# ScalarE loads one table set for both logarithm and exponential at the head of stages with norms

## The chip, the cores and the metric

The kernel runs on one core of a Trainium2 chip. A core has five engines with their own instruction streams: TensorE (PE in the profile), VectorE (DVE), ScalarE (ACT), GpSimd (POOL) and SyncE (SP), which here only issues transfers. The metric is the device time of one execution in microseconds; it is compared by the median of several runs.

## The reference, cut to what matters

One inference step runs two decoder layers on 512 prompt tokens and 64 sample tokens (8 requests of 8), 576 tokens in all, with a model width of 1024. Layer 0 mixes Mamba-2 heads with sparse attention heads, layer 1 mixes gated DeltaNet heads with dilated attention heads, and each layer ends in an MLP with a hidden width of 4096. What bears on the change is how often a root mean square stands in it:

```python
def rmsnorm(x, w):
    xf = x.astype(jnp.float32)
    y = xf * lax.rsqrt(jnp.mean(xf * xf, axis=-1, keepdims=True) + RMS_EPS)
    return (y * w.astype(jnp.float32)).astype(x.dtype)

def l2norm(x):
    xf = x.astype(jnp.float32)
    return xf * lax.rsqrt(jnp.sum(xf * xf, axis=-1, keepdims=True) + 1e-6)

# per layer
h = rmsnorm(x, norm_mix_pre);  x = x + rmsnorm(mixer(h), norm_mix_post)
h = rmsnorm(x, norm_mlp_pre);  x = x + rmsnorm(mlp(h), norm_mlp_post)
# mlp(h) = square(relu(h @ w1)) @ w2
# inside the mixers: silu(conv(...)), rmsnorm(y * silu(z)) behind the Mamba-2 scan, l2norm of the DeltaNet
# queries and keys, an rmsnorm of each DeltaNet head, softmax and sigmoid gates in the attention parts
```

## The kernel before

Activations lie transposed in SBUF, features on the 128 partitions and the 576 tokens along the free dimension, mostly handled as two halves of 288 tokens. Matrix products are done in three passes: each operand is split into a high part (a cast) and a low part (the difference), and high times high, high times low and low times high are summed in PSUM. For weights, ScalarE makes the high part of a 1 MB chunk (L283, `split_high`) and GpSimd the low part (L295, `split_low`). So TensorE has nearly all the work, and each norm is a place where it may have to wait for the other engines.

The program is a row of stages (`stage`, L101). A stage is one block in which every engine has its own list of instructions, written out by hand. The engines meet at a barrier between two stages; in the trace that wait is released by "PEq L114" or another sequencer at L114. Within a stage semaphores order the work, and an engine never runs ahead of its own list: whatever stands behind an instruction in the list waits for it.

A reciprocal root is computed on ScalarE as exp(-0.5 * ln(mean + eps)). Each of the two functions is looked up in a table set, and the sets that the toolchain picked for `Ln` and for `Exp` were different ones. Before an instruction whose function is not in the set that is loaded, the toolchain puts an ACT_TABLE_LOAD. It stands ahead of the instruction that carries the wait, so a load may run while ScalarE waits.

The places with such a pair, in order of time, are these:
- the first norm (`first_norm`: Ln L396, Exp L398), at 28 us;
- the norm behind the Mamba-2 scan (`inv_rms`: L312, L314), at 323 us;
- two layer tails (`layer_tail`, from 692 us and from 2311 us). A tail begins with the output product of the mixer, for which ScalarE and VectorE first split the activations (L2621, L2762). Then comes the norm of the mixer's output, the residual sum and the norm before the MLP (`chain_rms` L2289 and L2291, `chain_rms_both` L2300 and L2303; three pairs between 786 and 826 us), the MLP, and the norm behind it (around 1207 to 1260 us and 2807 to 2831 us). The steps of such a norm alternate between the engines: squares on ScalarE, their sums on VectorE (L2775) or GpSimd (L2342), the sum over the partitions as a product with ones on TensorE (L2275, L2281), Ln and Exp on ScalarE, the scaling on VectorE (L2352, L2313), the high part on ScalarE (L2362) and the low part on GpSimd (L2371), then the next product;
- the convolution stages of the DeltaNet part (`project_conv`, L825): ScalarE applies Silu to each of 12 channels, and `roots` (L915, L919) turns the sums of squares of the queries and keys into reciprocal roots, twice in each of two stages. The stage ends with the rows that go out (L963, then transfers of SP at L1039);
- the norm of the DeltaNet heads' output (`gdn_norm`, L3033 to L3040), twice.

The other functions that need a set of their own are Silu (L910, L1547, L1739, L2718), Sigmoid (L1656, L2941) and the Exp of softmax and decays.

Of the kernel before, what the change touches and what calls it, by code (L numbers as in the profile page):

```python
# [305 lines left out]
    return high_slot(K, i, kt * cols).rearrange("p (k n) -> p k n", k=kt), slot(K.WRr, n, RING, kt, cols)  # L306


def inv_rms(act, K, ss, n, summed, count, link):

    act.wait_ge(summed, count)
    act.activation(ss, ss, ACT.Ln, scale=1.0 / n, bias=K.eps[0:ss.shape[0], :]).then_inc(link, 1)  # L312
    act.wait_ge(link, 1)
    return act.activation(ss, ss, ACT.Exp, scale=-0.5)  # L314
# [9 lines left out]
def first_norm(nc, K, HW, rowp):  # L324
# [4 lines left out]
    with ExitStack() as ctx:  # L329
# [3 lines left out]
        with stage(nc, "small_turned", "small_out", "turned", "x_dve", "x_act", "sq_done", "added", "summed", "rs_link", "rs_done",  # L333
# [47 lines left out]

            @block.scalar
            def _(act):
                for i, r in enumerate((K.ssm_a_log, K.ssm_dt_bias, K.ssm_d)):
                    act.dma_start(rowp[:, i, :], r[0].partition_broadcast(P)).then_inc(heads_in, 16)
                for k in range(KT):
                    if k % 2:
                        act.wait_ge(turned, k + 1)
                        act.copy(K.XT[:, k, 0:TOK], K.PSF[:, (k % 3) * 1024:(k % 3) * 1024 + TOK]).then_inc(x_act, 1)
                    x_copied(act, k)  # L390
                    if k >= 2:
                        act.wait_ge(added, k - 1)
                    act.activation(SQ[:, k % 2, :], K.XT[:, k, 0:TOK], ACT.Square).then_inc(sq_done, 1)
                split_high(K, act, K.at["sconv"])
                act.wait_ge(summed, 1)
                act.activation(in_halves(RS[:]), K.PS[:, 6:8, 0:HALF], ACT.Ln, scale=1.0 / D, bias=K.eps[:]).then_inc(rs_link, 1)  # L396
                act.wait_ge(rs_link, 1)
                act.activation(RS[:], RS[:], ACT.Exp, scale=-0.5).then_inc(rs_done, 1)  # L398
                for k in range(KT):
                    act.wait_ge(h_done, k + 1)  # L400
                    act.copy(K.HH[:, k, 0:TOK], K.HT[:, k, 0:TOK]).then_inc(hi_done, 1)
                act.wait_ge(heads_in, 48)
                act.activation(rowp[:, 0, :], rowp[:, 0, :], ACT.Exp)
# [421 lines left out]
def project_conv(nc, K, name, first, n_ch, HW, bias, SX, keep, work, state, qk=None, decays=None, ahead=0):  # L825
# [17 lines left out]
    with stage(nc, f"{name}_raw", f"{name}_kept", f"{name}_tap", f"{name}_conv",  # L843
# [66 lines left out]
            act.activation(SX[:, u, 0:TOK], CO[:, u % 2, :], ACT.Silu).then_inc(silu_done, 1)  # L910

        def roots(act, i0):
            for i in (i0, i0 + 2):
                x = qk.RS[:, i:i + 2, :]
                act.activation(x, x, ACT.Ln, scale=1.0, bias=K.eps[:]).then_inc(logged, 1)  # L915
            for i in (i0, i0 + 2):
                x = qk.RS[:, i:i + 2, :]
                act.wait_ge(logged, i // 2 + 1)
                act.activation(x, x, ACT.Exp, scale=-0.5).then_inc(rooted, 1)  # L919
# [582 lines left out]
def ssm_gate(nc, K, Y, chunk):  # L1502

    with ExitStack() as ctx:
# [7 lines left out]
        with stage(nc, "z_silu", "z_used") as (block, z_silu, z_used):  # L1512
# [22 lines left out]

            @block.scalar
            def _(act):
                for i, (c, t) in enumerate(units):
                    if t == 0:
                        split_high(K, act, chunk + 2 * c + 1)  # L1540
                    if t == 1:
                        split_high(K, act, chunk + 2 * c + 2)
                    act.wait_ge(K.mm, product_at(c, t))
                    if i >= 2:
                        act.wait_ge(z_used, i - 1)
                    n = TILES[t][1]
                    act.activation(SZ[0:n, i % 2, :], K.PS[0:n, Z_BANKS[i % 8], :], ACT.Silu).then_inc(z_silu, 1)  # L1547
# [11 lines left out]
def ssm_norm(nc, K, Y, chunk):  # L1559

    with ExitStack() as ctx:
# [3 lines left out]
        with stage(nc, "sq_done", "rs_link", "rs_done", "h_ready", "t_done", "yt_copied", "nw_in") as (  # L1565
# [10 lines left out]
            def _(act):  # L1576
                act.dma_start(nw[:], K.ssm_norm_w[0].rearrange("(k p) -> p k", p=P),
                              allow_slow_non_contiguous=True).then_inc(nw_in, 16)
                for t in range(TT):
                    if t:  # L1580
                        act.wait_ge(sq_done, t)
# [127 lines left out]
def nsa_compress(nc, K, chunk, rows, pe_rows, w2, QT, KV, KTT, KCT, VC, VCZ, PCT, GT):  # L1709
# [16 lines left out]
    with stage(nc, "pe_turned", "k_turned", "k_copied", "turned", "t_copied", "hid_silu", "hid_turned", "hid_copied", "out_mm",  # L1726
# [8 lines left out]
        @block.scalar  # L1735
        def _(act):
            def hidden(kv):
                act.wait_ge(K.mm, K.end[chunk + 4 * kv + 3])
                act.activation(HSr[:, kv, :], K.PS[0:R, 2 + kv, 0:QW], ACT.Silu).then_inc(hid_silu, 1)  # L1739

            hidden(0)
            act.wait_ge(s_ready, 1)
            act.activation(flat, flat, ACT.Exp, scale=SCALE).then_inc(exp_done, 1)
            hidden(1)

        @block.tensor
        def _(pe):
# [658 lines left out]
def layer_tail(nc, K, layer, parts):  # L2406
# [25 lines left out]
    with ExitStack() as ctx:  # L2432
# [24 lines left out]
        with stage(nc, "a_high", "a_low", "x_back", "relu_done", "sq_done", "high_done", "low_done", "acc_done", "z_out",  # L2457
# [156 lines left out]

            @block.scalar
            def _(act):
                k0 = 0
                for c, kt in enumerate(parts):
                    split_high(K, act, mix + c)
# [280 lines left out]
def gdn_scalars(nc, K, chunk, C, HW):  # L2900

    U = TT * GH
    with ExitStack() as ctx:
# [12 lines left out]
        with stage(nc, "rows_in", "conv_in", "conv_turned", "padded", "ba_out", "ba_turned", "exp_in", "exp_out", "g_ready", "cum_mm",  # L2916
# [16 lines left out]
            def _(act):  # L2933
                split_high(K, act, chunk + 1)
                act.dma_start(rowp[:, 0, :], K.gdn_a_log[0].partition_broadcast(P)).then_inc(rows_in, 16)
                act.dma_start(rowp[:, 1, :], K.gdn_dt_bias[0].partition_broadcast(P)).then_inc(rows_in, 16)
                act.dma_start(C.nw[:], K.gdn_norm_w[0].unsqueeze(1), allow_slow_non_contiguous=True).then_inc(rows_in, 16)
                act.wait_ge(K.mm, K.end[chunk])
                act.copy(in_halves(BAT[:, 0:TOK]), K.PS[0:2 * GH, 4:6, 0:HALF]).then_inc(ba_out, 1)
                act.wait_ge(ba_turned, 1)  # L2940
# [62 lines left out]
def gdn_norm(nc, K, C, SX, high, N, h0, chunk):  # L3003
# [5 lines left out]
    with stage(nc, "squared", "summed", "logged", "rs_ready", "gated", "used") as (  # L3009
# [19 lines left out]

        @block.scalar  # L3030
        def _(act):
            for i in range(N):
                act.activation(RS[:, i, :], tiles[i], ACT.Square).then_inc(squared, 1)  # L3033
            act.wait_ge(summed, N)
# [22 lines left out]
def gdn_pair(nc, K, C, SX, bigs, S, pair, h_base, chunk):  # L3057
# [47 lines left out]
    with stage(nc, "pe_0", "pe_1", "act_0", "act_1", "dve_0", "dve_1", "pool_0", "pool_1", "s0_in", "dve_link") as (  # L3105
# [44 lines left out]

        @block.scalar
        def _(act):
            for a, b in enumerate(B):
                act.wait_ge(dves[a], DV["DT"])
                act.activation(b.E, b.A, ACT.Exp).then_inc(acts[a], 1)
# [834 lines left out]
```

## Time and profile before

| | |
|---|---|
| runs | 2847.41, 2852.86, 2851.79 us; median 2851.79 us |
| profiled execution | span 2847.2 us from the first to the last instruction; the page gives no other time for it, and the lowest run lies 0.2 us above this span |
| TensorE matmul busy | 2595.4 us, 91% |
| TensorE weight load busy | 2310.1 us, 81% |
| VectorE busy | 1234.6 us, 43% |
| ScalarE busy | 970.3 us, 34% |
| GpSimd busy | 917.2 us, 32% |
| DMA | 232.75 MB, 82 GB/s mean |
| granted TensorE clock | mean 0.947 of full speed |

TensorE is busy for nine tenths of the span and the others for well under half, so what another engine saves shows in the time only where TensorE, or a barrier, waits for it. Such places have to be found one by one in the timeline. In a timeline row the first number is the start in us, the second the duration in us (from the first start to the last end where several instructions are merged into one row, which "xN" tells); a bracket at its end holds the idle time before it and what released it.

### The profile page before, as it was taken

What the parts mean: (1) busy time and instruction counts of PE and PEld (TensorE: products, weight loads), DVE (VectorE), ACT (ScalarE), POOL (GpSimd) and SP (SyncE); (2) the same over time, 40 slices, a digit from 0 to 9 for tenths busy, and PEclk for the clock granted to TensorE, in tenths of its full rate; (3) what the DMA queues carried; (4) which work ended last, traced back from release to release, by engine and by line L of the source; (5) the groups of instructions that cost most, each with busy time, mean ns of one, the idle gap of its engine ahead of it and who ended that gap; (6) DMA issues with size and microseconds to landing.
All of it is one profiled execution on the core that took longest, in us unless ns stands there. A gap on an engine that the chain in (4) does not pass through costs nothing. (4 is left out here: it accounts for less than half of the span.)

```text
span 2847.2 us, 44477 instructions
## 1 busy us (share of the span) xinstructions
PE 2595.4 (91%) x18503; PEld 2310.1 (81%) x18503; DVE 1234.6 (43%) x2491; ACT 970.3 (34%) x1750; POOL 917.2 (32%) x454
## 2 busy tenths in 40 slices
PE   6889899997989999989988898889998888999997
PEld 5856696556979999988877887788775677999997
DVE  6785303775152222355544454440016445322225
ACT  4442221664251121253622362232125434312122
POOL 2351220332453333343244224422320015433331
PEclk9989998999999999989998899889999999999999
DMA  5312366330312222222201120112230542222221
GB/s 156 92 44 83 73 133 187 150 167 5 86 60 90 75 89 78 72 94 79 68 27 30 47 68 26 31 47 84 89 105 17 156 124 73 75 90 75 89 76 62
DMA packets 206679, 232.75 MB, mean 82 GB/s; under 512 B 40461, under 2 KB 165229, under 8 KB 205871
## 3 DMA queue, kind: packets, MB, share of 16 engines
q1 hardware_dynamic: 204398, 229.66, 26.1%
q8 instruction: 147, 2.41, 0.4%
q10 hardware_dynamic: 2080, 0.25, 0.1%
q14 instruction: 54, 0.43, 0.1%
HBM read 207.93 MB, written 48.35 MB: 90 GB/s over the span
## 5 line engine op out<-in xcount | busy, mean ns | idle before, releaser
L295 POOL TENSOR_TENSOR WRr<-WR,WH 128x2048 fp32r<-128x2048 f32 (+2 forms) x100 | 443.9, 4439 | 835.0 <-ACT WH L283 741.7
L2383 PE MATMUL PS<-HHr,WRr 128*128 128x288 f32 x1104 | 327.3, 296 | 0.0
L450 PE MATMUL PS<-YTr,WRr 128*128 128x288 f32 x1024 | 303.5, 296 | 0.0
L283 ACT CAST WH<-WR 128x2048 fp32r<-128x2048 f32 (+2 forms) x100 | 182.2, 1823 | 331.2 <-DMA WR<-in_mlp_w 142.1
L450 PE MATMUL PS<-HHr,WH 128*128 128x288 f32 (+1 forms) x896 | 273.1, 305 | 20.8 <-PEq L114 20.8
L450 PE MATMUL PS<-YTr,lt_WX 128*128 128x288 f32 x1408 | 282.0, 295 | 0.0
L450 PE MATMUL PS<-HTr,WH 128*128 128x288 f32 (+1 forms) x896 | 270.1, 301 | 0.0
L450 PE MATMUL PS<-HHr,WRr 128*128 128x288 f32 (+1 forms) x896 | 270.0, 301 | 0.0
L295 POOL TENSOR_TENSOR WRr<-WR,lt_WX 128x2048 fp32r<-128x2048 f32 x34 | 158.1, 4651 | 256.2 <-ACT lt_WX L283 256.2
L2383 PE MATMUL PS<-HHr,WH 128*128 128x288 f32 x800 | 237.4, 297 | 0.3 <-POOL WRr L295 0.3
L2383 PE MATMUL PS<-HTr,WH 128*128 128x288 f32 x800 | 237.0, 296 | 0.0
L450 PEld LDWEIGHTS PS<-YTr,lt_WX 128*128 128x128 f32 x1408 | 227.3, 188 | 0.1
L2383 PEld LDWEIGHTS PS<-HHr,WRr 128*128 128x128 f32 x1104 | 209.1, 189 | 0.0
L450 PEld LDWEIGHTS PS<-YTr,WRr 128*128 128x128 f32 x1024 | 192.1, 188 | 0.0
L450 PEld LDWEIGHTS PS<-HHr,WH 128*128 128x128 f32 (+1 forms) x896 | 173.0, 193 | 22.8 <-POOL WRr L295 16.2
L2797 DVE TENSOR_TENSOR YT<-YT 128x576 f32<-128x576 f32 x64 | 55.0, 859 | 276.6 <-ACT YT L2687 265.9
L450 PEld LDWEIGHTS PS<-HTr,WH 128*128 128x128 f32 (+1 forms) x896 | 173.0, 193 | 0.6
L450 PEld LDWEIGHTS PS<-HHr,WRr 128*128 128x128 f32 (+1 forms) x896 | 172.7, 193 | 0.6
L477 PE MATMUL PS<-WH,HHr 128*128 128x512 f32 (+2 forms) x400 | 155.9, 390 | 9.6 <-PEq L114 9.6
L477 PE MATMUL PS<-WRr,HHr 128*128 128x512 f32 (+2 forms) x400 | 153.7, 384 | 0.0
L477 PE MATMUL PS<-WH,HTr 128*128 128x512 f32 (+2 forms) x400 | 153.5, 384 | 0.0
L2687 ACT ACTIVATE YT<-PS 128x576 f32<-128x576 f32 x56 | 36.5, 653 | 339.5 <-PE PS L2383 339.5
(681 smaller groups left out, 5938.4 us busy)
## 6 DMA issues: line engine op xcount, KB each, us to landing
WR<-in_mlp_w SPq DMA_DIRECT2D x64, 1024.0 KB, 5.3
WR<-in_cd_w_in SPq DMA_DIRECT2D x34, 1024.0 KB, 5.3
out_dil_s<-in_cache_dil_kv SPq DMA_DIRECT2D x2, 7936.0 KB
WR<-in_ab_w_in SPq DMA_DIRECT2D x12, 1024.0 KB, 5.3
past_rows<-in_cache_nsa_kv SPq DMA_DIRECT2D x16, 256.0 KB, 3.5
WR<-in_ab_w_in SPq DMA_DIRECT2D x16, 256.0 KB, 4.6
WR<-in_nsa_ck_w SPq DMA_DIRECT2D x4, 1024.0 KB, 5.6
WR<-in_nsa_cv_w SPq DMA_DIRECT2D x4, 1024.0 KB, 5.7
```

Source lines behind the costliest of these rows:

```text
L283: act.copy(high_slot(K, i, used), K.WR[:, n % RING, 0:used]).then_inc(K.hi, 1)
L295: pool.tensor_tensor(K.WRr[:, n % RING, 0:used], K.WR[:, n % RING, 0:used], high_slot(K, i, used).bitcast(F32), ALU.subtract).then_inc(K.l ...
L450: last = pe.matmul(out, a, b, start=(n == 0), stop=(n == 3 * len(terms) - 1))
L477: last = pe.matmul(K.PS[0:rows, bank, 0:n], a, w[:, k, :], start=(half == 0 and k == 0 and m == 0), stop=(half == 1 and k == kt - 1 and m ...
L2383: last = pe.matmul(out, a[:, k, c], h[:, k, x], start=(n == 0), stop=(n == 3 * KT - 1))
L2687: act.activation(in_halves(whole(r, j)), both_halves(K, u % 2), ACT.Relu).then_inc(relu_done, 1)
L2797: dve.tensor_tensor(x, x, x, ALU.mult).then_inc(sq_done, 1)
```

## The change

A function `logs_and_exps` loads the set that holds both logarithm and exponential. It is called at the head of ScalarE's list in the first stage, in the norm behind the Mamba-2 scan (behind one transfer issue), in both layer tails and in the two stages of the DeltaNet output norm, and at the head of `roots`. In five other places a load of the Silu, Exp or Sigmoid table is written out ahead of a wait or of a copy. All other instructions keep their places.

```diff
@@ -306,6 +306,11 @@
     return high_slot(K, i, kt * cols).rearrange("p (k n) -> p k n", k=kt), slot(K.WRr, n, RING, kt, cols)
 
 
+def logs_and_exps(act):
+
+    act.preload_act_table_set("natural_log_exp_and_others")
+
+
 def inv_rms(act, K, ss, n, summed, count, link):
 
     act.wait_ge(summed, count)
@@ -381,6 +386,7 @@
 
             @block.scalar
             def _(act):
+                logs_and_exps(act)
                 for i, r in enumerate((K.ssm_a_log, K.ssm_dt_bias, K.ssm_d)):
                     act.dma_start(rowp[:, i, :], r[0].partition_broadcast(P)).then_inc(heads_in, 16)
                 for k in range(KT):
@@ -910,6 +916,7 @@
             act.activation(SX[:, u, 0:TOK], CO[:, u % 2, :], ACT.Silu).then_inc(silu_done, 1)
 
         def roots(act, i0):
+            logs_and_exps(act)
             for i in (i0, i0 + 2):
                 x = qk.RS[:, i:i + 2, :]
                 act.activation(x, x, ACT.Ln, scale=1.0, bias=K.eps[:]).then_inc(logged, 1)
@@ -1535,6 +1542,7 @@
 
             @block.scalar
             def _(act):
+                act.preload_act_table(ACT.Silu)
                 for i, (c, t) in enumerate(units):
                     if t == 0:
                         split_high(K, act, chunk + 2 * c + 1)
@@ -1576,6 +1584,7 @@
             def _(act):
                 act.dma_start(nw[:], K.ssm_norm_w[0].rearrange("(k p) -> p k", p=P),
                               allow_slow_non_contiguous=True).then_inc(nw_in, 16)
+                logs_and_exps(act)
                 for t in range(TT):
                     if t:
                         act.wait_ge(sq_done, t)
@@ -1738,10 +1747,14 @@
                 act.wait_ge(K.mm, K.end[chunk + 4 * kv + 3])
                 act.activation(HSr[:, kv, :], K.PS[0:R, 2 + kv, 0:QW], ACT.Silu).then_inc(hid_silu, 1)
 
+            act.preload_act_table(ACT.Silu)
             hidden(0)
+            act.preload_act_table(ACT.Exp)
             act.wait_ge(s_ready, 1)
             act.activation(flat, flat, ACT.Exp, scale=SCALE).then_inc(exp_done, 1)
+            act.preload_act_table(ACT.Silu)
             hidden(1)
+            act.preload_act_table(ACT.Exp)
 
         @block.tensor
         def _(pe):
@@ -2614,6 +2627,7 @@
 
             @block.scalar
             def _(act):
+                logs_and_exps(act)
                 k0 = 0
                 for c, kt in enumerate(parts):
                     split_high(K, act, mix + c)
@@ -2935,6 +2949,7 @@
                 act.dma_start(rowp[:, 0, :], K.gdn_a_log[0].partition_broadcast(P)).then_inc(rows_in, 16)
                 act.dma_start(rowp[:, 1, :], K.gdn_dt_bias[0].partition_broadcast(P)).then_inc(rows_in, 16)
                 act.dma_start(C.nw[:], K.gdn_norm_w[0].unsqueeze(1), allow_slow_non_contiguous=True).then_inc(rows_in, 16)
+                act.preload_act_table(ACT.Sigmoid)
                 act.wait_ge(K.mm, K.end[chunk])
                 act.copy(in_halves(BAT[:, 0:TOK]), K.PS[0:2 * GH, 4:6, 0:HALF]).then_inc(ba_out, 1)
                 act.wait_ge(ba_turned, 1)
@@ -3029,6 +3044,7 @@
 
         @block.scalar
         def _(act):
+            logs_and_exps(act)
             for i in range(N):
                 act.activation(RS[:, i, :], tiles[i], ACT.Square).then_inc(squared, 1)
             act.wait_ge(summed, N)
@@ -3150,6 +3166,8 @@
 
         @block.scalar
         def _(act):
+            if pair == 0:
+                act.preload_act_table(ACT.Exp)
             for a, b in enumerate(B):
                 act.wait_ge(dves[a], DV["DT"])
                 act.activation(b.E, b.A, ACT.Exp).then_inc(acts[a], 1)
```

ScalarE's list holds 62 table loads before and 33 after the change. The lists of the other engines have the same instructions in the same order.

ScalarE at the head of a layer tail, before (lt_AH is the high part of the mixer's output, HT the product, lt_SQ its squares):

```order
L114 UNCONDITIONAL_BRANCH
L2615 UNCONDITIONAL_BRANCH
L2621 CAST lt_AH<-YT 128x576 x16
L283 CAST WH<-WR 128x2048
L2631 COPY HT<-PS 128x576
L2632 ACTIVATE lt_SQ<-PS 128x576
```

The same place after the change:

```order
L114 UNCONDITIONAL_BRANCH
L2628 UNCONDITIONAL_BRANCH
L311 ACT_TABLE_LOAD
L2635 CAST lt_AH<-YT 128x576 x16
L283 CAST WH<-WR 128x2048
L2645 COPY HT<-PS 128x576
L2646 ACTIVATE lt_SQ<-PS 128x576
```

A load now stands in front of the first cast that the stage begins with.

ScalarE in the norm before the MLP of the tail, before (PS holds the sums over the partitions, eps the constant, HHr the high part of the normed activations):

```order
L2635 COPY HT<-PS 128x288
L2636 ACTIVATE lt_SQ<-PS 128x288
L283 CAST WH<-WR 128x2048
L2300 ACT_TABLE_LOAD
L2300 ACTIVATE PS<-PS,eps 128x288 x2
L2303 ACT_TABLE_LOAD
L2303 ACTIVATE PS<-PS 128x288 x2
L2362 CAST HHr<-HT 128x288 x8
L2329 ACTIVATE lt_SQ<-X 128x288 x8
L2659 ACTIVATE YT<-PS 128x288 x2
L2289 ACT_TABLE_LOAD
```

The same place after the change:

```order
L2649 COPY HT<-PS 128x288
L2650 ACTIVATE lt_SQ<-PS 128x288
L283 CAST WH<-WR 128x2048
L2313 ACTIVATE PS<-PS,eps 128x288 x2
L2316 ACTIVATE PS<-PS 128x288 x2
L2375 CAST HHr<-HT 128x288 x8
L2342 ACTIVATE lt_SQ<-X 128x288 x8
L2673 ACTIVATE YT<-PS 128x288 x2
L2302 ACTIVATE PS<-PS,eps 128x288
L2304 ACTIVATE PS<-PS 128x288
```

Three loads are gone, two in front of and behind the pair of logarithms and one ahead of the next; the cast of a weight chunk (L283) still stands in front of the first logarithm.

ScalarE at the end of a DeltaNet convolution stage, before (g_SX are the channels, g_RS the sums of squares, X the rows that go out):

```order
L910 ACTIVATE g_SX<-YT 128x576
L915 ACT_TABLE_LOAD
L915 ACTIVATE g_RS<-g_RS,eps 128x1152 x2
L919 ACT_TABLE_LOAD
L919 ACTIVATE g_RS<-g_RS 128x1152 x2
L910 ACT_TABLE_LOAD
L910 ACTIVATE g_SX<-YT 128x576
L963 COPY X<-PS 27x512 x3
L967 COPY g_QE<-PS 128x576 x2
```

The same place after the change:

```order
L916 ACTIVATE g_SX<-YT 128x576
L311 ACT_TABLE_LOAD
L922 ACTIVATE g_RS<-g_RS,eps 128x1152 x2
L926 ACTIVATE g_RS<-g_RS 128x1152 x2
L916 ACT_TABLE_LOAD
L916 ACTIVATE g_SX<-YT 128x576
L970 COPY X<-PS 27x512 x3
L974 COPY g_QE<-PS 128x576 x2
```

Of three loads two are left, and none stands between the logarithms and the exponentials.

## Rows read from the trace of the kernel before

**Rows 1.** Page, part 1: engine, busy us, share of the span, instructions.

```profile
PE 2595.4 (91%) x18503; PEld 2310.1 (81%) x18503; DVE 1234.6 (43%) x2491; ACT 970.3 (34%) x1750; POOL 917.2 (32%) x454
```

**Rows 2.** Groups by line, ScalarE: count, busy us, mean ns of one, idle before.

```profile
L910 ACT ACT_TABLE_LOAD x9 | 11.5, 1283 | 0.2
```

**Rows 3.** Timeline, ScalarE then TensorE, first norm.

```profile
30.52 1.28 ACT L398 ACT_TABLE_LOAD   x1
...
35.29 0.40 PE L377 MATMUL PS<-HHr,WH 128*16 128x288 f32 x1 [5.62 <-DVE HTr L432]
```

**Rows 4.** Timeline, ScalarE then TensorE, norm behind the Mamba-2 scan.

```profile
324.35 1.28 ACT L314 ACT_TABLE_LOAD   x1
...
326.69 1.09 PE L1610 MATMUL PS<-ident,YT 128*128 128x128 f32 x8 [1.83 <-DVE YT L1592]
```

**Rows 5.** Timeline, ScalarE, first attention stage.

```profile
484.43 1.28 ACT L2010 ACT_TABLE_LOAD   x1 [3.92 <-PEq L114]
```

**Rows 6.** Timeline, ScalarE then TensorE, head of tail 0.

```profile
692.39 9.28 ACT L2621 CAST lt_AH<-YT 128x576 fp32r<-128x576 f32 x16 [7.58 <-PEq L114]
...
694.00 0.58 PE L2494 MATMUL PS<-lt_AH,WH 128*128 128x288 f32 x1 [2.17 <-DVE YTr L2762]
```

**Rows 7.** Timeline, VectorE, GpSimd, TensorE, ScalarE, norms before the MLP of tail 0.

```profile
796.06 1.09 DVE L2775 TENSOR_TENSOR lt_SS<-lt_SS,lt_SQ 128x288 f32<-128x288 f32 x1 [1.18 <-ACT lt_SQ L2636]
...
803.94 4.50 POOL L295 TENSOR_TENSOR WRr<-WR,WH 128x2048 fp32r<-128x2048 f32 x1 [1.35 <-ACT WH L283]
...
808.83 6.59 POOL L2371 TENSOR_TENSOR HTr<-HT,HHr 128x288 fp32r<-128x288 f32 x8 [0.40 <-ACT HHr L2362]
...
808.90 0.58 PE L2396 MATMUL PS<-HHr,lt_WX 128*128 128x288 f32 x1 [4.68 <-ACT HHr L2362]
...
822.76 0.75 PE L2281 MATMUL PS<-lt_SS,ones 128*128 128x288 f32 x2 [1.97 <-POOL lt_SS L2342]
...
824.04 1.28 ACT L2291 ACT_TABLE_LOAD   x1
```

**Rows 8.** Timeline, ScalarE then VectorE, norm behind the MLP of tail 0.

```profile
1235.35 1.28 ACT L2303 ACT_TABLE_LOAD   x1
...
1228.01 5.43 DVE L2832 TENSOR_TENSOR lt_SS<-lt_SS,lt_SQ 128x288 f32<-128x288 f32 x2
```

**Rows 9.** Timeline, ScalarE, SP, TensorE, end of the first convolution stage.

```profile
1414.38 1.28 ACT L919 ACT_TABLE_LOAD   x1
...
1423.06 0.30 SPq L1040 DMA_DIRECT2D out_gdn_conv_s<-X  x1
...
1394.23 1.10 PE L887 MATMUL PS<-g_RS,ones 128*128 128x512 f32 x2 [0.97 <-ACT g_RS L941]
...
1423.92 1.36 PE L3252 MATMUL PS<-YT,ones 128*128 128x512 f32 x2 [3.70 <-PEq L114]
```

**Rows 10.** Timeline, ScalarE, GpSimd, TensorE, first DeltaNet output norm.

```profile
1589.16 2.41 ACT L3033 ACTIVATE YT<-g_SX 128x576 f32<-128x576 f32 x4 [8.11 <-PEq L114]
1602.01 1.28 ACT L3040 ACT_TABLE_LOAD   x1
...
1607.57 4.49 POOL L295 TENSOR_TENSOR WRr<-WR,WH 128x2048 fp32r<-128x2048 f32 x1 [39.01 <-ACTq L114]
...
1595.07 1.13 PE L3026 MATMUL PS<-YT,ones 128*128 128x512 f32 x2
...
1612.42 0.58 PE L450 MATMUL PS<-HHr,WH 128*128 128x288 f32 x1 [6.39 <-PEq L114]
```

**Rows 11.** Chain that ended last, end of the kernel: start us, us, what.

```profile
2829.47 0.02 issue
2829.48 1.28 ACT L2291
2830.77 0.01 issue
```

**Rows 12.** Stretches of time, `us, busy by engine, PEclk (granted TensorE clock), DMA`.

```profile
801.00:824.00 23.00, 14.71 (x83) 13.51 (x84) 14.14 (x25) 16.26 (x30) 18.95 (x18) 0.77 0.10 34
```

## The prediction

> **What bounds the kernel now.** I read the page first: TensorE is busy for 2595.4 of 2847.2 us, ScalarE for 970.3 [rows 1]. So time is to be had from a table load only where TensorE waits behind ScalarE, or where the barrier at the end of a stage does. The second view was the groups by line: all 62 table loads take 1283 ns each, whatever they load; the largest group stands in [rows 2]. With 29 fewer, ScalarE is busy 29 x 1.283 = 37 us less; that is the ceiling if every one of them stood on the path. The third view was the timeline around each load, on all engines, next to the list of TensorE's pauses (some 250 us in all). What one sees there is that a load ahead of a logarithm mostly runs while ScalarE waits for the sum from TensorE, since it stands ahead of the instruction that carries the wait. The load between logarithm and exponential can't hide in that way: its input is there when the logarithm ends.
>
> **Price of one load.** In the chain at the end of the kernel 0.02 us lie between the logarithm and the exponential's load, and 0.01 us between the load and the next activation [rows 11]. So an exposed load is worth 1.3 us by these rows. The Trainium skill (ScalarE: Activation LUTs, "What ACT_TABLE_LOAD costs") agrees on 1283 ns, but adds a drain of some 1380 ns to each switch, 2.66 us in all. No row here has such a second piece. By the page's figure, as an estimate, the sum below would come to some 28 us. I go by the rows.
>
> **The change part by part**, in order of time.
>
> 1. First norm. The logarithm's load runs while TensorE still sums, so it is worth nothing; the exponential's load is exposed, and TensorE waits 5.62 us there [rows 3]. The new load at the head of the list runs while ScalarE waits for its first input. -1.3 us.
>
> 2. Silu's load ahead of the first weight cast in the stage behind the Mamba-2 scan, and Sigmoid's ahead of a copy: neither has a pause of TensorE of over 1 us behind it that it feeds; 0. If the cover were gone each would cost 1.3.
>
> 3. Norm behind the scan. ScalarE starts on the squares as soon as the stage opens, so the new load delays them by 1.3. Both old loads stood between squares and result, with TensorE waiting 1.83 us at the end [rows 4]: 2.6 less. Net -1.3.
>
> 4. The Silu and Exp loads of the compression stage stood ahead of their waits in the list already: 0. But Exp's load for the attention stage moves to the end of the stage before. There the old one stood at the head [rows 5], beside VectorE's first maximum, for which its exponential waits too. It is bounded by 0 and 1.3; since VectorE has a product of TensorE to wait for first, I take -0.3.
>
> 5. Head of each layer tail. Here the change speaks against itself. ScalarE's first cast begins at once when the stage opens, and VectorE and TensorE follow within 1.6 us; TensorE has nothing else to do and waits 2.17 us for it [rows 6]; tail 1 begins in the same way. The new load stands in front of that cast, behind the barrier. Queued behind it are all 16 (in tail 1, 12) casts. +1.3 twice, +2.6.
>
> 6. Norms before the MLP, two tails. The first pair: the exponential gets done 1.3 earlier, but VectorE then waits anyway for the square of a product that TensorE has yet to finish (1.18 us at 796.06), so nothing is gained. The second pair loses both loads, 2.6 us of ScalarE. But what follows needs GpSimd, and that is busy with the low part of a weight chunk until 803.94 + 4.50 = 808.44; its first low part of the activations starts at 808.83, so it can come 0.4 earlier and not 2.6. From there GpSimd works without a pause to the sum that TensorE waits for at 822.76. Since squares come earlier I add 0.3 for places where GpSimd waited for them. The third exponential's load, at 824.04, is exposed: 1.3 [rows 7]. -2.0 in each tail, -4.0. Bounds: 1.7 for each tail, without the 0.3, and 3.9 with all three loads.
>
> 7. Norm behind the MLP of tail 0. The first exponential is awaited by nobody (VectorE scales only after a later product). The second, at 1235.35, is exposed; GpSimd gives 0.3 of it on, VectorE's list the rest, up to the next sum over the partitions [rows 8]. The third is covered by two products that TensorE still has queued. -1.3, bounds 0.3 and 2.6.
>
> 8. Convolution stages, two with two root blocks each. ScalarE loses one load per block. The end of the stage follows ScalarE: at 1414.38 the load, then exponentials, Silu, the rows that go out, then six transfer issues of SP up to 1423.06 + 0.30, and TensorE starts the next stage at 1423.92 after 3.70 us [rows 9]. The load at 1414.38 is worth 1.3. The load of the first block lies 25 us earlier, with waits of ScalarE for TensorE and VectorE in between. They pass it on nearly whole, I think: TensorE stands still for 0.97 us behind that block [rows 9], and VectorE is held there by GpSimd's work on a chunk, which a cast of ScalarE starts. -2.5 a stage, -5.0; bounds 1.3 and 2.6 a stage.
>
> 9. DeltaNet output norm, twice. The squares start as soon as the stage opens, so they come 1.3 later; but TensorE reaches the sums only at 1595.07, 3.5 us after they end. The old load ahead of the logarithm was hidden, the one at 1602.01 isn't: behind it stand the exponentials, a weight cast and GpSimd's low part of it, which ends the stage at 1612.06 [rows 10]. -1.3 each, -2.6.
>
> 10. Norm at the very end: the load at 2829.48 lies in the chain that ended last [rows 11]. -1.3. The pair before it is covered by products, as in part 7.
>
> The sum: 1.3 + 1.3 + 0.3 + 4.0 + 1.3 + 5.0 + 2.6 + 1.3 = 17.1 gained, 2.6 lost, so -14.5 us. The profiled execution's span is 2847.2 us, 4.6 below the median of the runs; I take the difference off the median: 2851.8 - 14.5 = 2837.3 us. A measurement here tells about 0.2%, 5.7 us, from no change.
>
> **What no row prices** is TensorE's clock. Between 801 and 824 us, with pauses of 4.68 and 1.97 us [rows 7] among others, its mean is 0.77 [rows 12]: after such a pause products run at the lower level (1.2 GHz) for some 4 us, at twice the time each, which costs up to 2 us. The change makes eight pauses shorter and four longer (the heads of both tails, to 3.5 us, and the pause at 822.76 in both, since TensorE gets there earlier). If every one of the four costs a whole slow stretch more, that is +8; if four of the shorter ones lose theirs, -8. I take 0 between these ends, because pauses of 2 us already have it.
>
> **Rivals.**
> - The first root block's load stays where it is: only the second counts, or SP's issues or TensorE end the stage. For it: ScalarE waited for TensorE in between. Against it: TensorE's pause of 0.97. With 1.3 to 0.5 a stage, the sum is some 4 smaller: 2841.
> - Longer pauses cost clock. Part 5 and the two of part 6 give +8: 2845. For it speaks the 0.77; against it that the pauses had their slow stretch before.
> - No change that can be measured, because the waits behind ScalarE are taken over by GpSimd and SP nearly everywhere, as GpSimd does in part 6: only parts 1, 3, 9 and 10 remain, -6.5, with +2.6 of part 5: -3.9, 2848.
> - The change saves twice as much. Each exposed load would hold its engine for longer than its row, so the 12 exposed ones less the 2 new ones count 1.3 more each: -28, 2824. Against it: the 0.01 and 0.02 us on both sides of a load [rows 11]. This is what the Trainium skill's drain (same page and section) would make of it.
> - Slower than before. VectorE and GpSimd get in each other's way: at 1228.01 two sums of VectorE that take 0.45 each otherwise take 5.43, while GpSimd works on a weight chunk [rows 8], which takes it 4.5 [rows 7]. The change shifts ScalarE and VectorE by 1 to 3 us against GpSimd at about ten places. A VectorE sum that started just before such an operation and falls just behind its start costs 4.5. It decides from the fifth such hit: 5 x 4.5 = 22.5 makes -14.5 into +8, 2860. Against it: there are as many places at which a hit can go away.
>
> **Chances.** The forecast 0.64, with a range of its own of 2832 to 2843; first root block not passed on 0.15; clock 0.08; no change 0.06; twice as much 0.03; slower 0.04. The range that should hold 8 in 10 goes from 2830, which takes in the upper bounds of parts 6 to 8 (3.8, 1.3 and 0.2 more), to 2845, the clock's case. Faster by over 0.2% is the forecast, the first rival, half of the clock's and the double saving: 0.86. Within it are the other half and the case of no change: 0.10. Slower: 0.04.
>
> **What the profile after would show.** 33 loads, ScalarE's busy time at some 933 us. Exponentials that start 0.02 us behind their logarithms. At the head of both tails a table load and TensorE's pause at 3.5 us instead of 2.2. TensorE's pause ahead of the first MLP product down from 4.7 to some 2, but the pause behind it (1.97) up to 3 or more, with GpSimd's low parts 0.4 earlier only. The pause at the end of the convolution stages down from 3.7 to about 2 or less. The forecast is wrong if that pause is the same, if the first pair in a tail gives time, or if TensorE's busy time grows by over 5 us with the same number of products, which would be the clock.

## The result, and the profile after

The first comparison gave 2827.34 us for the changed kernel (median of 4 runs, 2826.99 to 2828.41) and 2849.86 us for the one before (4 runs, 2847.41 to 2852.86), a ratio of 0.9918 with a 95% interval of 0.9904 to 0.9932. That is 22.5 us less where 14.5 were forecast, and the time lies below the range, which began at 2830.

This size did not hold. Both kernels were run often beside the experiments. All executions that have their mean granted clock recorded:

| kernel | executions | mean us (standard deviation) | mean granted clock | at a clock of 0.950, from the fit below |
|---|---|---|---|---|
| before | 57 | 2847.3 (4.2) | 0.9484 | 2844.5 |
| after | 16 | 2829.3 (4.4) | 0.9514 | 2831.8 |
| combined (below) | 12 | 2824.6 (3.6) | 0.9531 | 2830.2 |

The change is worth 18.0 us (two standard errors: 2.5), and the mean of 2829.3 still lies 0.7 us below the range. A straight line through all executions of all kernels, with a constant for each kernel, gives 1.8 us for each 0.001 of granted clock. At equal clock the change is worth 12.7 us (two standard errors: 1.7); the other 5.3 come with the higher clock (0.0030 more at 1.8 us for each 0.001). That clock does not come from the session in which a kernel was run: in the two sessions in which both ran side by side again, the mean was 0.9475 before and 0.9505 after, and 0.9490 and 0.9518.

Page, part 1, of the first trace after the change. It answers to [rows 1]; the span is 2825.6 us against 2847.2.

```profile
PE 2585.8 (92%) x18503; PEld 2306.0 (82%) x18503; DVE 1235.2 (44%) x2491; ACT 932.7 (33%) x1721; POOL 914.9 (32%) x454
```

ScalarE is busy 37.6 us less, as worked out, and its count is down by the 29 loads. Span less TensorE's busy time is what TensorE stands still: 2847.2 - 2595.4 = 251.8 before and 2825.6 - 2585.8 = 239.8 after, 12.0 less. The other 9.6 us of this pair of traces are TensorE's busy time for the same 18503 products, so they are the clock.

The best place to see that is one that the change does not touch. TensorE, head of the first dilated attention stage, of before and then of after; the bracket is the pause and who ended it.

```profile
2125.30 1.65 PE L3529 MATMUL PS<-d_K,X 64*128 64x256 f32 x5 [1.66 <-DVE f_nm L3616]
2130.85 1.86 PE L3529 MATMUL PS<-d_K,X 64*128 64x256 f32 x5 [2.46 <-DVE f_nm L3616]
```

```profile
2110.72 0.91 PE L3547 MATMUL PS<-d_K,X 64*128 64x256 f32 x5 [1.66 <-DVE f_nm L3634]
2114.85 1.02 PE L3547 MATMUL PS<-d_K,X 64*128 64x256 f32 x5 [2.46 <-DVE f_nm L3634]
```

The pauses are the same to 0.01 us, and the same five products take 1.65 us in one trace and 0.91 in the other. Stretches of the same place, `us, busy by engine, PEclk, DMA`: before and then after.

```profile
2124.00:2136.00 12.00, 7.78 (x32) 5.51 (x34) 7.43 (x27) 4.06 (x9) 0.00 (x0) 0.57 0.80 289
```

```profile
2108.00:2120.00 12.00, 6.28 (x52) 4.70 (x54) 9.47 (x34) 5.63 (x13) 0.00 (x0) 1.00 0.89 314
```

A granted clock of 0.57 means mostly the lower level (1.2 GHz), 1.00 the upper one (2.4 GHz). From 2100 to 2200 us of before this alone makes 5.4 us: 20.5 us of that stretch are at the lower level in before and 6.8 in after.

To keep the two causes apart I cut the traces at the same products of TensorE and took the time between them, and within it the sum of TensorE's pauses of over 0.15 us (worked out from the timelines of all traces; the limits are times of before):

| stretch | before, 2 traces: us (pauses) | after, 3 traces: us (pauses) | pauses changed by |
|---|---|---|---|
| 300-400 | 99.96, 100.00 (7.9, 7.9) | 98.91, 98.95, 98.93 (6.6, 6.6, 6.6) | -1.3 |
| 690-780 | 89.73, 90.32 (3.1, 3.1) | 91.32, 90.88, 91.33 (4.4, 4.4, 4.4) | +1.3 |
| 780-900 | 120.08, 120.64 (10.8, 11.1) | 117.70, 118.16, 117.66 (8.3, 8.4, 8.3) | -2.6 |
| 1200-1300 | 99.98, 100.59 (13.9, 14.8) | 97.66, 97.65, 97.61 (13.2, 13.6, 13.2) | -1.0 |
| 1560-1700 | 140.01, 139.25 (11.5, 11.5) | 135.78, 138.01, 138.00 (9.3, 9.3, 9.3) | -2.2 |
| 2100-2200 | 100.99, 95.98 (13.0, 12.8) | 95.59, 96.68, 97.73 (13.0, 11.9, 12.9) | none |
| 2380-2450 | 70.08, 69.21 (14.3, 13.8) | 66.69, 66.36, 66.27 (11.3, 11.0, 11.6) | -2.8 |
| 2450-2800 | 349.90, 349.94 (0, 0) | 349.90, 349.94, 349.94 (0, 0, 0) | none |

With the pauses below 0.15 us the changes in 780-900 and 2380-2450 are -3.0 us each.

### The profile page after: what moved, and what is told of

Same layout as the page of the kernel before. It is cut to its first block and busy times, and to the rows that moved or that the text cites. A ratio compares the mean times of both kernels' runs of the same rounds, so it can differ in the third digit from the quotient of the medians.

```text
span 2825.6 us, 44448 instructions
## 1 busy us (share of the span) xinstructions
PE 2585.8 (92%) x18503; PEld 2306.0 (82%) x18503; DVE 1235.2 (44%) x2491; ACT 932.7 (33%) x1721; POOL 914.9 (32%) x454
## 5 line engine op out<-in xcount | busy, mean ns | idle before, releaser
L283 ACT CAST WH<-WR 128x2048 fp32r<-128x2048 f32 (+2 forms) x100 | 182.2, 1823 | 318.4 <-DMA WR<-in_mlp_w 142.1
L456 PEld LDWEIGHTS PS<-HHr,WH 128*128 128x128 f32 (+1 forms) x896 | 171.4, 191 | 20.2 <-POOL WRr L295 13.6
L2396 PEld LDWEIGHTS PS<-HHr,WH 128*128 128x128 f32 x800 | 150.8, 188 | 0.9 <-POOL WRr L295 0.8
```

The lines of the kernel that those rows point to most:

```text
L283: act.copy(high_slot(K, i, used), K.WR[:, n % RING, 0:used]).then_inc(K.hi, 1)
L456: last = pe.matmul(out, a, b, start=(n == 0), stop=(n == 3 * len(terms) - 1))
L2396: last = pe.matmul(out, a[:, k, c], h[:, k, x], start=(n == 0), stop=(n == 3 * KT - 1))
```

## The experiments

Each "idle" below is span less TensorE's busy time of the profiled execution. Interval means 95%.

**The same kernels again.** Both were run unchanged, for second and third traces and more times.

> The kernel after the change, as it was, a second time. Theory (the placed loads give some 14 us, and a further 7 us come from TensorE's clock, because the same pauses fall otherwise against the moments at which it is switched): the clock part differs from one execution to the next, so the median is 2827 to 2832 us, and the second trace has the pauses of the first to 0.1 us, but at least three of the stretches at the lower level (1.2 GHz) start or end elsewhere, above all between 2105 and 2170 us. Rival (the clock part belongs to the change, it comes back in each run): 2827 to 2828 us and the same stretches.

Measured: 2830.66 us (6 runs, 2821.76 to 2840.14), ratio 0.9938, interval 0.9918 to 0.9959; span 2831.1, idle 238.8. Most pauses are the same: of some 170 over 0.3 us, 136 agree to 0.015 us in all three traces of after, and 149 to 0.1 us. The others move; the largest difference is at the product that starts at 1922 us in before (0, 0 and 1.40 us). The clock is not the same: where the first trace has 3.4 us at 1.2 GHz at 666 us and 13.7 at 686, this one has 20.5 at 678; the 17.1 us at 1765 are 13.7 at 1770; and at 2119, where the first has none, there are 3.4. The first theory holds, though not for every pause: this kernel alone spreads over 18 us.

> The kernel before the change, unchanged, for a second trace of it and more of its times. Theory: TensorE's pauses come back to 0.1 us (span less TensorE's busy time 251.8 us, as in the first trace, within 1.5), the granted clock differs between executions, and the time with it, by about 1.9 us for each 0.001 of mean clock. The stretch of 14 us at 1.2 GHz between 2124 and 2141 us, which the first trace of after lacks, is elsewhere or shorter in this one. Rival (that stretch belongs to the kernel before): it is here again.

Measured: 2846.58 us (12 runs), ratio 0.9999 to its like, interval 0.9985 to 1.0014; idle 252.7. Between 2124 and 2142 us one stretch of 3.4 us at 1.2 GHz is left of two with 13.7 us, so they were not a property of the kernel. In the trace of `first_later` (below), a kernel with the change, two stretches with 13.7 us stand there again.

> The kernel after the change a third time, for its mean over many executions. The difference to before that does not hang on one chip's clock: mean 2829 us with 2 us to either side, 18 us under before, of which 13 are pauses and 5 the clock; span less TensorE's busy time 239.3 within 1.5 us. Rival (the first result, -22.5 us, is the true size): mean 2825 to 2827.

Measured: 2828.87 us (6 runs), ratio 0.9936, interval 0.9923 to 0.9948; idle 241.7, a little outside the 1.5 us expected. The mean of these six and the ten before is 2829.3. The first result's size, -22.5, falls. Its interval (at least 19.4 us less) does not hold the 18.0 of all executions: four executions of after happened to lie within 1.4 us of each other, where all sixteen spread over 18.

**What one load costs.** Ahead of `logs_and_exps(act)` at the head of the tail:

```diff
+                if layer == 0:
+                    act.preload_act_table(ACT.Silu)
```

In the second kernel that load stands twice, with a `logs_and_exps(act)` between: three loads more than after.

> After the change, with one more table load (Silu's set) in front of that at the head of tail 0. If a load costs what its row shows, TensorE's pause at the head of the tail grows from 3.46 to 4.75 us and the time by 1.3, to 2828.6. If each switch also has a drain as long as the load (the rival that saves twice as much), the pause grows by 2.6 and the time to 2830. If the moments at which the clock is switched decide, the time is off this line by up to 5 us to either side, although all later pauses are the same.

> After the change, with three more table loads in front of that at the head of tail 0. By the rows: pause 3.46 + 3.85 = 7.3 us, time +3.85, 2831.2. With a drain of the same length: pause 11.2, time 2835. If the clock's moments decide, off the line of 1.28 us a load by up to 5 us to either side, and not by the same as with one more load.

Measured, TensorE's first product of tail 0 in after, with one and with three more loads:

```profile
694.20 0.58 PE L2507 MATMUL PS<-lt_AH,WH 128*128 128x288 f32 x1 [3.46 <-DVE YTr L2776]
```

```profile
690.13 0.58 PE L2507 MATMUL PS<-lt_AH,WH 128*128 128x288 f32 x1 [4.75 <-DVE YTr L2778]
```

```profile
696.60 0.58 PE L2507 MATMUL PS<-lt_AH,WH 128*128 128x288 f32 x1 [7.33 <-DVE YTr L2782]
```

That is 1.29 us a load, what its row shows and no more. The rival that saves twice as much falls by its mechanism, although its 2824 was the nearest number. The Trainium skill (ScalarE: Activation LUTs, "What ACT_TABLE_LOAD costs") adds a drain of some 1380 ns to each switch; these pauses do not bear that out for loads behind a barrier, nor do those ahead of which a load between logarithm and exponential is gone (7.69 to 6.41 us at the end of the kernel). The times, 2828.92 and 2830.27 us, ratios 0.9938 (0.9924 to 0.9953) and 0.9939 (0.9927 to 0.9952), tell little of this. The first fits all three lines that were expected; the second lies 0.9 us under the line of the rows and 4.7 under that of the drain.

**Head of tail 1.**

```diff
-                logs_and_exps(act)
+                if layer == 0:
+                    logs_and_exps(act)
```

> After the change, without the load at the head of tail 1; the set with both functions is still there from the output norm. ScalarE's 30 loads further ahead stay. By part 5 of the prediction: TensorE's pause at the head of that tail back from 3.6 to 2.3 us, the time 1.3 us under that of the unchanged kernel after (2827.3), so 2826.0. If the clock answers to the longer pause as well: 1.3 to 3 us under it. Rival (the load is no loss there, since TensorE waits for VectorE's split anyway): pause and time as they were.

The first product of tail 1:

```profile
2290.75 0.58 PE L2507 MATMUL PS<-lt_AH,WH 128*128 128x288 f32 x1 [2.33 <-DVE YTr L2777]
```

The pause is 3.61 in after, 2.33 here: part 5 was right on the pause. The time is 2830.21 us (6 runs), ratio 0.9946, interval 0.9929 to 0.9963, which is above the 2826.0 expected and tells nothing on 1.3 us.

**Why the first norm gave nothing.** VectorE, the first two scalings, and TensorE's pause in after:

```profile
31.06 3.19 DVE L434 SCALAR_TENSOR_TENSOR HT<-X,normT,fn_rs 128x576 f32<-128x576 f32 x2 [3.93 <-ACT fn_rs L404]
```

```profile
35.16 0.40 PE L382 MATMUL PS<-HHr,WH 128*16 128x288 f32 x1 [5.63 <-DVE HTr L438]
```

They start 1.48 earlier than before (32.54), but take 3.19 us instead of 1.84, and the pause is 5.63 against 5.62 [rows 3]. GpSimd is at work on a low part from 28.40 to 32.90. The test holds that work back:

```diff
                 pool.wait_ge(padded, 2)
                 pool.tensor_copy(K.HTr[:, :, TOK:TP], K.HT[:, :, TOK:TP]).then_inc(padded, 1)
+                pool.wait_ge(h_done, 2)
                 split_low(K, pool, K.at["sconv"])
```

> After the change, with GpSimd's low parts of the first weights held until VectorE has made its first two scaled rows of the first norm. Theory (part 1 of the prediction fails because VectorE's first scaling stands still while GpSimd works on the 128x2048 low part, so that the 1.3 us saved on ScalarE are waited out on VectorE): the first two scalings, 3.19 us together in after, take 1.5 to 1.7, and ScalarE's first cast of a scaled row (HHr) starts at 31.9 us and not at 33.55. TensorE gets its weights later and pays that back, so its pause there grows: 2 to 5 us longer. Rival (VectorE is slow there for a reason of its own): the two scalings take 3.2 us as before, starting at 31.06.

VectorE and GpSimd in that kernel:

```profile
30.51 1.55 DVE L434 SCALAR_TENSOR_TENSOR HT<-X,normT,fn_rs 128x576 f32<-128x576 f32 x2 [3.93 <-ACT fn_rs L404]
...
33.67 5.05 DVE L438 TENSOR_TENSOR HTr<-HT,HHr 128x576 fp32r<-128x576 f32 x1
```

```profile
32.15 5.96 POOL L295 TENSOR_TENSOR WRr<-WR,WH 128x128 fp32r<-128x128 f32 x2 [18.89 <-DVE HT L434]
```

With GpSimd out of the way the two take 1.55, and the subtraction that now falls beside it takes 5.05 instead of 0.75. (One run, 2839.44 us; TensorE's pause is 9.22, since its weights come later.) So VectorE stands until GpSimd is done: GpSimd's two end at 38.11 us, the subtraction at 38.72. The Trainium skill (SBUF — State Buffer, "SBUF: two separate sides") has this as an exclusive lock on a shared port pair, held for a whole instruction; the trace agrees.

**Why the convolution stages gave half.** ScalarE and SP's queue at the end of the first such stage, in after; it answers to [rows 9].

```profile
1411.40 1.34 ACT L974 COPY g_QE<-PS 128x576 f32<-128x576 f32 x2
```

```profile
1412.09 0.37 SPq L262 DMA_DIRECT2D WR<-in_cd_w_in  x1
1412.50 0.46 SPq L1046 DMA_DIRECT2D out_gdn_conv_p<-X  x1
...
1414.58 0.30 SPq L1047 DMA_DIRECT2D out_gdn_conv_s<-X  x1
```

SP's last weight transfer waits for TensorE's last product and is issued from 1412.09 to 1412.46. The six transfers of the rows stand behind it and take 2.4 us, whatever ScalarE has saved. Before the change, SP's list looked so:

```profile
1420.25 0.37 SPq L262 DMA_DIRECT2D WR<-in_cd_w_in  x1
1421.33 0.28 SPq L1039 DMA_DIRECT2D out_gdn_conv_p<-X  x1
```

There SP did wait for ScalarE, whose rows were done at 1421.30, but only for 0.7 us (1420.62 to 1421.33). More than that no load could give at the stage's end, and of it 0.35 went back, since the six issues take 2.38 us after and took 2.03 before. The test gives three of the six to ScalarE, behind its last copy, and takes them out of SP's list:

```diff
+                act.wait_ge(kept_out, 3)
+                for to, at, n in cols:
+                    act.dma_start(out_s[:, :, at:at + n].rearrange("b s c -> (b s) c"), rows[3:27, to:to + n]).then_inc(K.state_out, 16)
```

> After the change, with three of the six transfer issues at the end of each DeltaNet convolution stage on ScalarE's queue, behind its last copy, and three left to SP. Theory (part 8 of the prediction fails because SP issues the six behind a weight transfer that waits for TensorE's last product, so that they take 2.4 us whatever ScalarE saves): TensorE's pause at the head of the next stage goes from 3.36 to 2.3 us, twice, 2 us in all, and the time is 2 us under that of after, which is less than the clock makes from run to run. Rival (the barrier waits for ScalarE's exponentials, Silu and copies): the pause grows, since ScalarE has 1.2 us more to do, to 4.5.

TensorE's first product of the next stage, in after and in this kernel:

```profile
1415.42 1.10 PE L3270 MATMUL PS<-YT,ones 128*128 128x512 f32 x2 [3.36 <-PEq L114]
```

```profile
1414.57 1.10 PE L3278 MATMUL PS<-YT,ones 128*128 128x512 f32 x2 [2.24 <-PEq L114]
```

The pause is 2.24 us (2.13 in the second stage) instead of 3.36, although ScalarE has more to do: SP's list was the limit. Time 2827.92 us (6 runs), ratio 0.9923, interval 0.9906 to 0.9939. Idle is 240.0, no less than in after: the pause at 1922 us that comes and goes is 1.41 in this trace.

**One part alone.** Before, with only the load at the head of the tails.

> The kernel before, with the load of the set with both functions at the head of the two layer tails and no other part of the change. Theory: the places add up as their pauses do. Span less TensorE's busy time 252.3 us (mean of two traces of before), +1.3 at the head of each tail, -2.6 and -2.7 in the norms before the MLP, -1.0 behind the MLP of tail 0 and -1.3 at the end: 247.3. The clock gives 1.7 us more behind the MLP of tail 0 and a little in tail 1. Time about 7 us under before, 2840.5. Rival (the clock's share goes with all parts of the change together): 5 us under before, 2842.5, and the stretch at 1.2 GHz between 1230 and 1260 us stays 17 us long.

Measured: 2840.80 us (12 runs), ratio 0.9977, interval 0.9963 to 0.9991; idle 248.4 where 247.3 was expected; the stretches at 1.2 GHz between 1230 and 1265 us last 10.2 us. The places behave as in the whole change: 91.20, 117.82 and 97.36 us for the stretches 690-780, 780-900 and 1200-1300. The part from 400 to 690 us took 297.36 us instead of 290.3 and 291.4, in a piece where nothing was changed. VectorE and GpSimd there:

```profile
663.55 4.29 DVE L2229 COPY q_E<-q_Pc 128x4 f32<-128x4 f32 x1
```

```profile
663.31 4.50 POOL L295 TENSOR_TENSOR WRr<-WR,WH 128x2048 fp32r<-128x2048 f32 x1 [14.87 <-ACT WH L283]
```

The same copy takes 0.17 us elsewhere. It began just behind GpSimd's instruction and ended with it, and TensorE's pause behind it is 4.70 us instead of 0.59. So one execution's trace can hold such a hit and the next not, and this pause, not the tails, keeps the idle time above the 247.3.

**One load put back.** Between the logarithms and the exponentials behind the MLP of tail 0, in after, and with it a load of the common set ahead of the next wait, which is hidden (it runs from 1252.42 to 1253.70, the next logarithm waits for TensorE's sum until 1255.40):

```diff
     act.wait_ge(C.link, 3)
+    if again:
+        act.preload_act_table(ACT.Exp)
     for b in range(2):
...
+                    logs_and_exps(act)
                     chain_rms(K, act, Z, 1, 4)
```

> After the change, with a load of Exp's own set put back at one place, between the logarithms and the exponentials behind the MLP of tail 0, and a load of the set with both ahead of the next wait for TensorE. Theory: one load there costs twice, once as a pause and once by the clock. TensorE's pause goes from 2.10 back to 3.38 us, the time at 1.2 GHz between 1225 and 1265 us from 10.2 back to 17.1 us, and the products of before's 1200 to 1300 us take 100.0 to 100.6 us instead of 97.65. Rival (the clock has nothing to do with this pause): 98.95 us, and 10.2 us at 1.2 GHz. Everything ahead of it as in after.

Stretches of after and then of this kernel:

```profile
1225.00:1265.00 40.00, 29.28 (x186) 26.77 (x185) 28.41 (x43) 21.11 (x45) 28.33 (x20) 0.87 0.24 86
```

```profile
1225.00:1265.00 40.00, 27.41 (x163) 25.57 (x164) 28.31 (x43) 23.00 (x44) 27.67 (x20) 0.79 0.24 86
```

TensorE there:

```profile
1235.83 0.58 PE L2411 MATMUL PS<-HHr,lt_WX 128*128 128x288 f32 x1 [3.38 <-ACT HHr L2377]
```

The pause is 3.38 instead of 2.10, the clock 0.79 instead of 0.87, and 1200-1300 takes 100.43 us instead of 97.65: one exposed load of 1.28 us costs 2.8, of which 1.7 are pauses (14.9 against 13.2) and 1.1 slower products. The 17.1 us at 1.2 GHz are there in this kernel (one trace) and both traces of before; in every trace with the shorter pause but one (13.7, the second trace of combined) there are 10.2. The whole kernel ran in 2829.28 us (4 runs), ratio 0.9940, interval 0.9925 to 0.9956: the time alone would have shown nothing.

**A better version.** The shared issues, and the load of the tails where it costs nothing: in tail 0 behind the 16 casts, in tail 1 left out.

```diff
-                logs_and_exps(act)
                 k0 = 0
...
                     k0 += kt
+                if layer == 0:
+                    logs_and_exps(act)
```

> After the change, with the shared issues of rows_shared, the load of tail 0 moved behind the 16 casts that the stage begins with, and none in tail 1 (the set is there from the output norm). Theory: the pauses at the heads of the tails 3.46 to 2.2 and 3.61 to 2.33 us, those at the end of the convolution stages 3.36 to 2.3, all others the same: span less TensorE's busy time 239.3 (mean of two traces of after) less 4.6, 234.7. Time 4.6 us under after at the same clock, so a median of 2822 to 2827 us. Rival (the load behind the casts delays the copies of the output product): one of the next pauses of that tail grows by up to 1.3 us.

> The combined kernel (tail 0's load behind the casts, none in tail 1, the rows' transfer issues shared) a second time, beside after on the same chip. 4 to 5 us under after: the four pauses are 4.8 us shorter together. Rival (the time does not follow, since the clock takes it back): within 2 us of after.

```profile
693.85 0.58 PE L2515 MATMUL PS<-lt_AH,WH 128*128 128x288 f32 x1 [2.17 <-DVE YTr L2785]
```

Measured: 2823.67 us (6 runs), ratio 0.9911, interval 0.9893 to 0.9928, and again 2824.32 us (6 runs), ratio 0.9929, interval 0.9914 to 0.9944. Idle 235.8 both times, 4.3 under the mean of after (240.1); the pauses at the heads of the tails are 2.17 and 2.33 again, and no later one grew in the first trace. In the second the pauses from 780 to 900 us are 10.1 us instead of 8.6, while only 6.8 us there are at 1.2 GHz instead of 13.7, and the stretch takes the same time (117.88 and 117.72 us): a faster TensorE waits longer for the others. The mean time is 4.7 us under that of after (two standard errors: 3.0). At equal clock 1.6 of them are left (two standard errors: 2.1), less than the 4.3 of idle time; why these two differ is open.

## Why the prediction was wrong

The step that failed is "What no row prices": it took the clock as 0 between -8 and +8, and the clock is worth -5.3. The forecast time, 2837.3, lies 8.0 us above the mean of 2829.3. Of these, 4.5 are the base: the sum was taken off the median of three runs, 2851.8, and the mean of the kernel before is 2847.3. (The profiled execution's span, 2847.2, is near that mean by luck: a span leaves out some 1.8 us of the time, as 2825.6 against 2827.38 shows for after.) The other 3.5 are the clock's 5.3, less 1.8 by which the terms fell short: 12.7 at equal clock instead of 14.5. That they came so near is in part luck too, since parts 1 and 8 gave 3.7 us less than forecast and part 6 gave 1.4 more. The difference of the first result, -22.5, is 4.5 us larger than the true one by chance of eight executions: the four of after lie 1.8 us under their mean, and the four of before 2.7 over theirs.

| part | forecast | measured, by the pauses | |
|---|---|---|---|
| 1 first norm | -1.3 | 0 | wrong: VectorE stands behind GpSimd |
| 2 Silu, Sigmoid ahead | 0 | no pause of over 1 us changed | right, not tested alone |
| 3 norm behind the scan | -1.3 | -1.3 | right |
| 4 attention's Exp | -0.3 | ahead of the first product behind it 0.81 and 0.82 to 0.47, 0.40 and 0.45: -0.3 or a little more | right |
| 5 heads of the tails | +2.6 | 3.46 - 2.17, 3.61 - 2.33 = +2.6 | right, shown by taking it away |
| 6 norms before the MLP | -4.0 | -2.6 and -2.8 | mechanism right, first pair wrong |
| 7 behind the MLP, tail 0 | -1.3 | -1.0 | right |
| 8 convolution stages | -5.0 | -1.3 each | wrong: half |
| 9 output norm | -2.6 | 6.39 to 5.11, twice: -2.6 | right |
| 10 end norm | -1.3 | 7.69 to 6.41: -1.3 | right |
| sum | -14.5 | -11.9; by idle -12.2 | |

Part 6 said that the first pair gives nothing. The pause ahead of the second sum over the partitions went from 4.18 to 3.56 us in tail 0 and from 6.71 to 5.46 in tail 1, so it did; the prediction had named this as a sign of being wrong. The second pair came as said: GpSimd's first low part starts at 808.31 instead of 808.83 [rows 7], held by the weight chunk up to 808.35, and the pause at the first MLP product goes from 4.68 to 2.10. The pause behind it did not grow to 3 us or more but is 2.16, with a new one of some 0.5 between the two. How before's time splits between the two pauses changes from trace to trace (4.68 and 1.97, then 3.98 and 2.65), their sum hardly (6.65, 6.63).

Part 8 said that ScalarE ends the stage and that both loads count. The first one did: TensorE's pause of 0.97 behind that block is gone. The second hardly did: the pause of 3.70 [rows 9] became 3.36, where the prediction had named about 2 or less and an unchanged pause as a sign of being wrong. Over all traces of the two kernels and both stages it is 3.66 to 3.81 before and 3.34 to 3.58 after. I read SP's issues as something that follows ScalarE, and did not look at what stood ahead of them in SP's own list, which left 0.7 us to gain.

The clock. The forecast had named this case, "if four of the shorter ones lose theirs, -8", and set both signs equal. It also read [rows 12] too small: "some 4 us" at 1.2 GHz after each pause, where the trace of before has 10.2 us from 803.4 and 3.4 from 823.9. One place is shown: behind the MLP of tail 0 the shorter pause loses 6.8 us at 1.2 GHz in every trace of after, and the load put back brings them back; that is 1.1 us of slower products. Around the norms of tail 1 (2380-2450) it is 17.1 us in both traces of before and 13.7 or 10.2 in all twelve with shorter pauses, which was not tested by putting a load back. For the other 4 us or so I have no such test. In the stretches from 1300 to 1400 and from 1700 to 1800 us of before, the clock was on average higher in the traces after the change, but it also differs from one trace of the same kernel to the next by as much; what each shortened pause gives there stays open.

The rivals: the one on the first root block had the wrong block; longer pauses cost no clock that can be seen, since the heads of the tails (690-780: 91.2 after, 90.0 before, means) changed by their pause alone, and with three more loads that stretch takes 95.0 us, 3.8 more for 3.87 us of pause; VectorE and GpSimd newly got in each other's way once in every trace of after (part 1) and once in that of `tails_alone`, not five times.

## What to carry to other kernels

Find an exposed table load by asking what runs between its end and the next instruction, and then who else holds the next engine: of ten places two were already held, once by GpSimd's instruction and once by a queue of transfer issues that waited for TensorE itself. Put a load behind work that the others wait for, never ahead of it, and leave it out where the set is still there. Where executions of one kernel differ by 18 us, judge an edit of 1 us by TensorE's pause at the place, once two traces of one kernel agree on it (four of five do, to 0.015 us), and let many runs decide only on the sum.

## What the runs showed of the hardware that was not expected

The granted clock is not a property of the program alone: the same list of instructions, with pauses that sum to 235.2, 234.1 and 237.1 us, ran with 274.2, 291.3 and 283.5 us at 1.2 GHz in the three traces of after, and with 305.1 and 289.4 in the two of before. At 1.8 us for each 0.001 of mean clock it explains most of the spread of single executions (their standard deviation of 4.2 to 4.4 us falls to 2.7 once it is taken out). And a pause can cost more than itself: 1.28 us more of it behind the MLP of tail 0 cost 2.8 us when it was put back, and 2.3 and 2.9 us in the two traces of before against the first of after.
